# Recurrence of the HGRN2 mixer, pairs 0 and 1: four runs of small matmuls in place of seven

## What is computed

```
def chunk_step(state, inp):          # 8 heads, keys and values 128 wide
    qc, kc, vc, gc = inp             # gc = log of the forget gate
    b = jnp.cumsum(gc, axis=2)
    o_inter = einsum('bhck,bhkv->bhcv', qc * exp(b), state)
    diff = b[:, :, :, None, :] - b[:, :, None, :, :]
    decay = exp(where(causal, diff, -inf))
    scores = einsum('bhtk,bhsk,bhtsk->bhts', qc, kc, decay)
    o_intra = einsum('bhts,bhsv->bhtv', scores, vc)
    ...
```

## Time and profile before

| | us |
|---|---|
| runs | 2103.4 to 2104.62, median 2104.47 |
| profiled execution | 2104.02 |
| its span, first to last instruction | 2101.6 |
| busy in the span: PE, DVE, ACT, POOL | 2090.5, 1013.5, 742.4, 1144.2 |
| pair 0 of the recurrence | 73.9 to 113.1 |
| pair 1 | 113.1 to 157.8 |

### The profile page before, as it was taken

The page is one execution under the profiler, slowest core; times in us unless marked ns, Lnnn a source line. Parts: engine busy times, 40 slices in busy tenths (PEclk is TensorE's granted clock), DMA queues, the critical chain, the costliest instruction groups (busy, mean ns, idle before and its releaser), DMA issues.

```text
span 2101.6 us, 28243 instructions
## 1 busy us (share of the span) xinstructions
PE 2090.5 (99%) x11210; PEld 1737.6 (83%) x11210; DVE 1013.5 (48%) x1192; ACT 742.4 (35%) x862; POOL 1144.2 (54%) x821
## 2 busy tenths in 40 slices
PE   9999999999999999999999999999999999999998
PEld 7888788888888889888888888888888888888887
DVE  6367555555123365634555333744477544454126
ACT  6335542222224445533222233515433332212234
POOL 6677455555555433365555555544566555555553
PEclk9999999999999999999999999999999999999999
DMA  5212132222232222242222222222222222222321
GB/s 197 84 62 82 41 120 97 86 97 100 100 116 96 98 69 93 81 140 97 86 98 100 100 100 101 102 98 101 99 89 94 98 100 100 100 89 104 117 100 60
DMA packets 33209, 204.39 MB, mean 97 GB/s; under 512 B 3688, under 2 KB 6504, under 8 KB 9456
## 3 DMA queue, kind: packets, MB, share of 16 engines
q1 hardware_dynamic: 32896, 203.13, 28.0%
q10 hardware_dynamic: 240, 0.23, 0.0%
HBM read 200.19 MB, written 2.10 MB: 96 GB/s over the span
## 4 chain that ended last, share of the span: by engine, by line
PE 96%; DVE 2%; ACT 1%; issue 0%; DMA 0%; POOL 0%; SPq 0%; DVEq 0%; ACTq 0%
PE bank L1958 96%; DVE x L1841 0%; DMA h<-x_t 0%; DVE sgate L1890 0%; PE bank L2343 0%; ACT w_hi L776 0%; PE bank L2231 0%; DVE h L1891 0%; POOL first_wlo L721 0%; DVE ssq L1915 0%; PE bank L2370 0%; ACT sgate L776 0%; DVE aqk L1631 0%; DVE score_pair L1495 0%; ACT rstd L776 0%
## 5 line engine op out<-in xcount | busy, mean ns | idle before, releaser
L654 POOL TENSOR_TENSOR w_lo<-raw,w_hi 128x512 fp32r<-128x512 f32 x676 | 977.3, 1476 | 861.9 <-ACT w_hi L776 861.9
L1958 PE MATMUL bank<-u_hi,w_hi 128*128 128x512 f32 (+1 forms) x1936 | 753.2, 389 | 0.1
L1958 PE MATMUL bank<-u_lo,w_hi 128*128 128x512 f32 (+1 forms) x1936 | 749.5, 387 | 0.0
L776 ACT ACTIVATE w_hi<-raw 128x2048 fp32r<-128x2048 f32 x185 | 354.2, 1915 | 915.5 <-PE bank L1958 911.7
L1958 PE MATMUL bank<-u_hi,w_lo 128*128 128x512 f32 (+1 forms) x1936 | 482.2, 387 | 0.0
L1958 PEld LDWEIGHTS bank<-u_hi,w_hi 128*128 128x128 f32 x1936 | 363.6, 188 | 74.7 <-ACTq L1190 0.5
L1958 PEld LDWEIGHTS bank<-u_lo,w_hi 128*128 128x128 f32 x1936 | 363.6, 188 | 73.9 <-issue 0.2
L1958 PEld LDWEIGHTS bank<-u_hi,w_lo 128*128 128x128 f32 x1936 | 362.5, 188 | 74.6
L1958 PE MATMUL bank<-act_hi,w_hi 128*128 128x512 f32 x528 | 205.4, 389 | 0.0
L1958 PE MATMUL bank<-act_lo,w_hi 128*128 128x512 f32 x528 | 205.4, 389 | 0.0
L1329 DVE TENSOR_TENSOR h<-h,bank 128x512 f32<-128x512 f32 x48 | 30.8, 683 | 300.2 <-PE bank L1958 300.2
(11 more groups left out here) (293 smaller groups left out, 2109.2 us busy)
## 6 DMA issues: line engine op xcount, KB each, us to landing
raw<-wall SPq DMA_DIRECT2D x185, 1024.0 KB, 4.9
out_t<-h SPq DMA_DIRECT2D x8, 256.0 KB, 2.5
h<-x_t SPq DMA_DIRECT2D x3, 512.0 KB, 7.5
first_raw<-wall SPq DMA_DIRECT2D x6, 256.0 KB, 7.4
av_moved<-av SPq DMA_DIRECT2D x14, 64.0 KB, 2.1
h<-x_t SPq DMA_DIRECT2D x2, 256.0 KB, 3.9
first_raw<-wall SPq DMA_DIRECT2D x4, 128.0 KB, 3.8
lmask_f<-lmask_in SPq DMA_DIRECT2D x1, 512.0 KB
```

The source lines that it names most:

```text
L654: ins = nc.gpsimd.tensor_tensor(w_lo[:, s, c], raw[:, s, c], w_hi[:, s, c].bitcast(F32), ALU.subtract)
L776: return nc.scalar.activation(out, in_, func, **k)
L1958: return nc.tensor.matmul(out, lhsT, rhs, start=start, stop=stop, skip_group_check=True)
```

## The change

In pairs 0 and 1, levels 2 and 3, 4 and 5, and 6 and 7 each share one run on PE. The lower level of a run reads `q_dec` and `key` as before. The upper one reads two new buffers, `q_next` and `key_next`, which hold the operands of level l with the folding of level l-1 already in. `next_queries(p, l)` and `next_keys(p, l)` on VectorE make them ahead of the run: of every four quarters of a block the two that the upper level reads, one copied, one multiplied by a decay, 128x256 each. The folds in place stay, for the later levels and for the states; they now come two at a time behind the run. PE waits for both new buffers before the lower level of a run. The slices of a pair are dealt out anew, 24 as before. `key_next` is cleared once. The semaphore of the query folds is split in two, `first_dec` for the product that starts a pair and `qdec_ready` for the folds.

Cut to its core:

```diff
-LEVEL_SLICES = ((0, 4, 4, 4, 3, 3, 3, 3), (0, 4, 4, 4, 3, 3, 3, 3), (0, 4, 3, 3, 3, 3, 2, 3), (0, 3, 2, 3, 2, 2, 2, 1))
+TWO_LEVELS = 2
+LEVEL_SLICES = ((0, 3, 3, 3, 3, 4, 3, 5), (0, 3, 3, 3, 3, 4, 3, 5), (0, 4, 3, 3, 3, 3, 2, 3), (0, 3, 2, 3, 2, 2, 2, 1))
...
+        key_next = place("key_next", "a", 4, [P, 2 * S])
+        q_next = place("q_next", "a", 12, [P, 2 * S])
...
+        def levels_at(p, l):
+
+            if p >= TWO_LEVELS or l < 2:
+                return (l,)
+            return (l - 1, l) if l % 2 else ()
+
+        def next_at(p, l):
+            return (STEPS // 2 - 1) * p + l // 2
+
+        def quarters_of(t, l):
+
+            b = t.rearrange("p (n c) -> p n c", c=4 * span_of(l))
+            return [b[:, :, k * span_of(l):(k + 1) * span_of(l)] for k in range(4)]
...
+        def quarter_end(p, l, k):
+
+            t = decay_at(p, l).rearrange("p (n four) -> p n four", four=4)
+            return t[:, :, k:k + 1].to_broadcast([P, S // (2 * span_of(l)), span_of(l)])
...
             for p in range(PAIRS):
                 lo_piece(6 + 3 * p, 0, 4) if p == 0 else lo_piece(6 + 3 * p, 2, 4)
-                if p < PAIRS - 1:
+                if p < TWO_LEVELS:
+                    fold_keys(p, 1)
+                    lo_piece(7 + 3 * p, 0, 4)
+                    fold_keys(p, 2)
+                    fold_keys(p, 3)
+                    if p:
+                        head_lower(2 * p - 2)
+                    lo_piece(8 + 3 * p, 0, 4)
+                    fold_keys(p, 4)
+                    fold_keys(p, 5)
+                    decays(p + 1)
+                    lo_piece(9 + 3 * p, 0, 2)
+                    if p:
+                        head_lower(2 * p - 1)
+                    fold_keys(p, 6)
+                    fold_keys(p, 7)
+                elif p < PAIRS - 1:
...
-                tt(q_dec[p % 2][:], query[:], forget[:], ALU.mult).then_inc(qdec_ready, 1)
+                tt(q_dec[p % 2][:], query[:], forget[:], ALU.mult).then_inc(first_dec, 1)
...
                 dve.wait_ge(lev_done, 2 * STEPS * p + 2 * l + 2)
-                dve.wait_ge(qdec_ready, STEPS * p + l)
-                if l > 1:
+                if l == 1:
+                    dve.wait_ge(first_dec, p + 1)
+                else:
+                    dve.wait_ge(qdec_ready, (STEPS - 1) * p + l - 1)
                     dve.wait_ge(decay_made, (STEPS - 1) * p + l - 1)
                 high = halves_of(q_dec[p % 2], l)[1]
                 tt(high, high, ends_of(p, l)[0], ALU.mult).then_inc(qdec_ready, 1)
+
+            def next_queries(p, l):
+
+                dve.wait_ge(qdec_ready, (STEPS - 1) * p + l - 1)
+                dve.wait_ge(decay_made, (STEPS - 1) * p + l - 1)
+                to, t = quarters_of(q_next[:], l), quarters_of(q_dec[p % 2][:], l)
+                cp(to[2], t[2]).then_inc(qnext_ready, 1)
+                tt(to[3], t[3], quarter_end(p, l, 2), ALU.mult).then_inc(qnext_ready, 1)
+
+            def next_keys(p, l):
+
+                dve.wait_ge(kend_ready, (STEPS - 1) * p + l - 1)
+                dve.wait_ge(decay_made, (STEPS - 1) * p + l - 1)
+                to, t = quarters_of(key_next[:], l), quarters_of(key[p % 2][:], l)
+                cp(to[1], t[1]).then_inc(knext_ready, 1)
+                tt(to[0], t[0], quarter_end(p, l, 1), ALU.mult).then_inc(knext_ready, 1)
...
             for e in range(2):
-                ins = nc.vector.memset(scores_of_pair[e][:], 0.0)
-            ch.step(ins)
+                nc.vector.memset(scores_of_pair[e][:], 0.0)
+            ch.step(nc.vector.memset(key_next[:], 0.0))
...
+            for p in range(TWO_LEVELS):
+                fold_queries(p, 1)
+                next_queries(p, 2)
+                take_products(p)
+                take_level(p, 1)
+                next_keys(p, 2)
+                head_step(p, 1)
+                if p:
+                    gate_in(p - 1)
+                head_step(p, 2)
+                for l in (3, 5):
+                    fold_queries(p, l - 1)
+                    fold_queries(p, l)
+                    if l == 5:
+                        head_step(p, 5)
+                    next_queries(p, l + 1)
+                    take_level(p, l - 1)
+                    take_level(p, l)
+                    next_keys(p, l + 1)
+                    if l == 3:
+                        head_step(p, 3)
+                        forget_in(p + 1)
+                        head_step(p, 4)
+                        forgets(p + 1)
+                    else:
+                        keys(p + 1)
+                query_in(p + 1)
+                head_step(p, 6)
+                take_level(p, 6)
+                take_level(p, 7)
+                first_decay(p + 1)
+                head_step(p, 7)
+                if p:
+                    head_normed(2 * p - 2)
+                fold_queries(p, 6)
+                fold_queries(p, 7)
+            for p in range(TWO_LEVELS, PAIRS):
...
-                n = 2 * STEPS * p + 2 * l + a
-                q = query if l == 0 else q_dec[p % 2]
+                later = p < TWO_LEVELS and l > 1 and l % 2
+                q = query if l == 0 else q_next if later else q_dec[p % 2]
+                k = key_next if later else key[p % 2]
+                if a == 0 and p < TWO_LEVELS and l > 1:
+                    pe.wait_ge(qnext_ready, 2 * next_at(p, l))
+                    pe.wait_ge(knext_ready, 2 * next_at(p, l))
                 if a == 0 and l == 0:
                     pe.wait_ge(query_ready, p + 1)
                     pe.wait_ge(key_ready, p + 1)
-                elif a == 0:
-                    pe.wait_ge(qdec_ready, STEPS * p + l)
-                    if l > 1:
+                elif a == 0 and not later:
+                    if l == 1:
+                        pe.wait_ge(first_dec, p + 1)
+                    else:
+                        pe.wait_ge(qdec_ready, (STEPS - 1) * p + l - 1)
                         pe.wait_ge(kend_ready, (STEPS - 1) * p + l - 1)
...
-                    level(p, l, 0)
-                    level(p, l, 1)
+                    for run in levels_at(p, l):
+                        level(p, run, 0)
+                        level(p, run, 1)
```

More of the change, by code:

```diff
@@ L347, in build @@
         lev_free = sem("lev_free")
+        first_dec = sem("first_dec")
         qdec_ready = sem("qdec_ready")
+        qnext_ready = sem("qnext_ready")
+        knext_ready = sem("knext_ready")
         kend_ready = sem("kend_ready")
@@ L705, in fold_keys @@
                     pool.wait_ge(decay_made, (STEPS - 1) * p + l - 1)
+                    pool.wait_ge(kend_ready, (STEPS - 1) * p + l - 1)
                 low = halves_of(key[p % 2], l)[0]
@@ L1575, in _, with head_step @@
             for e in range(2):
-                ins = nc.vector.memset(scores_of_pair[e][:], 0.0)
-            ch.step(ins)
+                nc.vector.memset(scores_of_pair[e][:], 0.0)
+            ch.step(nc.vector.memset(key_next[:], 0.0))
             cp(sel_r[:], sel[:]).then_inc(sel_ready, 1)
             ch.settle()
-            for p in range(PAIRS):
+            def head_step(p, l):
+                if p:
+                    for e, step in HEAD_STEPS[l]:
+                        tail(2 * p - 2 + e, step)
+            for p in range(TWO_LEVELS):
[30 more added lines that the diff above has]
+                head_step(p, 7)
+                if p:
+                    head_normed(2 * p - 2)
+                fold_queries(p, 6)
+                fold_queries(p, 7)
+            for p in range(TWO_LEVELS, PAIRS):
                 for l in range(1, STEPS):
@@ L2209, in level @@
                             at = slice(CUT * b, CUT * (b + 1))
-                            ins = mm(PB[5][at, CUT * c:CUT * (c + 1)], near(key[p % 2], c)[:, at], near(q, c)[:, at])
+                            ins = mm(PB[5][at, CUT * c:CUT * (c + 1)], near(k, c)[:, at], near(q, c)[:, at])
                     elif span_of(l) >= CUT:
-                        ins = early_late_beside(l, near(key[p % 2], c), near(q, c), c)
+                        ins = early_late_beside(l, near(k, c), near(q, c), c)
                     elif span_of(l) >= LEAST_BLOCK:
                         for b in range(P // (2 * span_of(l))):
-                            ins = early_late(near(level_bank(l), c // 2), near(key[p % 2], c), near(q, c),
+                            ins = early_late(near(level_bank(l), c // 2), near(k, c), near(q, c),
                                              span_of(l), b, (c % 2) * P // 2)
@@ L2219, in level @@
                             at, to = slice(CUT * b, CUT * (b + 1)), c * P // 2 + b * CUT // 2
-                            ins = mm(level_bank(l)[at, to:to + CUT // 2], near(key[p % 2], c)[:, at],
+                            ins = mm(level_bank(l)[at, to:to + CUT // 2], near(k, c)[:, at],
                                      halves_of(near(q, c)[:, at], l)[1])
@@ L2243, in outputs @@
                 pe.wait_ge(states_ready, hd + 1)
```

(2 more changed lines are left out.)

## The result

| | before | after |
|---|---|---|
| median of the runs, us | 2103.43 | 2114.62 |
| lowest to highest (6 runs each) | 2103.21 to 2104.62 | 2108.39 to 2116.64 |
| profiled execution, its span | 2104.02, 2101.6 | 2115.07, 2113.3 |
| pair 0 of the recurrence | 39.17 | 45.29 |
| pair 1 | 44.67 | 50.20 |

The ratio is 1.0049, with a 95% interval of 1.0039 to 1.0059. The forecast was 2107.6, its range ended at 2110.6. The forecast stood on a median of 2104.47 for the kernel before, of three runs; over the six runs it is 2103.43. So the forecast change of +3.1 us is to be held against a measured +11.2. The span grew by 11.7 us, and all of it is in the two pairs that were changed: 6.12 in pair 0 and 5.53 in pair 1 (a pair is read from the start of its first `query,key` matmuls to the start of the next pair's).

A forecast was written before the change was run, and what follows sets the result against it. PE, busy 99%, was taken as the bound; -0.7 + 1.1 + 0 + 1.6 + 0.4 + 0.7 = +3.1 us on the profiled 2104.02, with 0.45 for the median, gave 2107.6, range 2104.3 to 2110.6.

The forecast's parts named there:

- merging, pair 0: Pair 0 goes from seven groups of small matmuls to four; three crossings saved, 0.72 us, at most 0.99.
- merging, pair 1: Pair 1 keeps seven groups because tail matmuls now stand alone between slices; 0 saved, bounds 0 and 0.99 us.
- places 1 and 3: PE waits before merged runs of pair 0 while DVE finishes `next_keys`: 1.1 us at run {2,3}, 1.6 at run {6,7}.
- places 2 and 4: PE waits 0 at run {4,5} of pair 0, and 0.4 us for the states at `outputs(0)` of pair 1.
- place 5: `keys_by_token(1)`, pair 1: PE waits 0.7 us for `head_taken(0)`, behind `next_keys` on DVE; 3.2 with two pieces in between.
- The price of a crossing: On PE, going from wide matmuls to small ones and back around a separate run costs 0.24 us.
- The price of the new DVE instructions: Each 128x256 copy or product costs 0.3 to 0.42 us, plus 0 to 1.27 where POOL streams.
- the fold that took 2.07: First fold of the queries on DVE, 2.07 us in place of 0.69, read as waiting for POOL's key fold.

The follow-up runs named there:

- half block: The changed kernel with three of ten warm-up matmuls replaced by 35 tiny ones, moving later PE code 128 instructions on: 2110.84 us, ratio 1.0029.
- half block with `head_taken(0)` early: The changed kernel with code moved 128 instructions on by tiny warm-up matmuls and `head_taken(0)` put ahead on DVE in pair 1: 2106.54 us, ratio 1.0008.
- `head_taken(0)` early: The changed kernel with `head_taken(0)` in pair 1 put ahead of `next_queries(1, 4)` and the two `take_level` on DVE: 2109.23 us, ratio 1.0023.
- pair 0 alone: The changed kernel with merged runs only in pair 0, pair 1 having the code of before: 2109.26 us, ratio 1.0022.
- the shifted kernel before: The kernel of before with one warm-up matmul replaced by 16 tiny ones, moving code 60 instructions on: 2104.25 us, ratio 1.0007.

## Why the prediction was wrong

Per pair, with the experiment from which each term is read:

| term | forecast | measured |
|---|---|---|
| merging, pair 0 | -0.7 | -0.8: 38.64 - 39.17 = -0.53, with 0.29 of wait in it |
| merging, pair 1 | 0 | -0.6: 44.76 - 44.67 = +0.09, with 0.65 of wait in it |
| places 1 and 3, run {2,3} and {6,7} of pair 0 | +1.1, +1.6 | +0.3, 0 |
| places 2 and 4 | 0, +0.4 | 0, 0 |
| place 5, `keys_by_token(1)` | +0.7 | +4.3 |
| slow clock behind it | not in the sum | +1.6 |
| pause inside run {2,3} | not in the sum | +3.9 |
| slow clock behind it | not in the sum | +2.4 |

The two measured pairs without losses are those of the half block (pair 0) and of the half block with `head_taken(0)` early (pair 1). The terms add up to 11.1 of the 11.65; the rest, half a microsecond, I can't place.

**What held.** The price of a crossing: 0.24 us three times is 0.72, and pair 0 without the pause saves 0.8. The price of the new DVE instructions: 0.3 to 0.43 alone and up to 1.5 beside a piece, by turns, as said of the fold that took 2.07. Which wait is new in pair 1, and its mechanism: place 5, with the sentence "If the pieces of the next panel reach POOL before `next_keys`, two of 1.27 go in between: 3.2". That is what happened, and I took 0.7.

**Place 5, a term mis-sized.** PE came when the forecast said: `outputs(0)` starts at O = 131.13 and PE arrives at 141.43 - 4.34 = 137.09, O + 6.0 (forecast O + 5.9). DVE's chain was to end at O + 6.7 and ended at O + 10.2. By its steps: the folds O + 3.0 (2.6); `next_queries` O + 4.8 (3.4), since its product lost a turn to `sum_lo`, a step of the tail that GpSimd had at 134.34 and that my chain left out; the levels O + 6.8 (5.3); `next_keys` O + 9.5 (6.0), with two pieces. The value between the ends was chosen as if the pieces were spread over the span. They start together when ScalarE has rounded the next panel, at 137.82, and `next_keys` starts at 137.88. With the upper end, which had its ground in the same trace, the forecast would have been 2110.1.

**The step that failed.** "The matmuls stay, their number and shapes too" and "The changed semaphore counts cost nothing" were read as: PE has nothing new to pay for inside a merged run. That term was put at nothing without a reason. But the trace of before has no run like these but one, levels 0 and 1, in which 256 instructions pass in 1.3 us, and I took from it that such a run is free anywhere. Whether it is depends on where the block of code ends. I gave no bound to it, from either side, and it is the largest single loss of the result, 3.9 us of waiting for code and 2.4 of slow clock behind it. The sentence that would have shown the forecast wrong, "a wait of over 2.5 us before any run of pair 0", came true inside a run instead.

**What every wait costs again.** The forecast priced a wait at its length. The two long ones cost 3.9 and 2.4, and 4.3 and 1.6, since the wide matmuls behind start 0.427 apart for a while. The experiments widen that: the pauses of 2.0 to 2.25 lost 1.2 to 1.7 us more behind them, that of 2.55 lost 2.5, those of 3.9 to 4.2 lost 1.3 to 2.5. So the second loss is 1.2 to 2.5 us whatever the length of the first. Waits up to 1.1 us, as the one of the earlier trace rows in pair 3 and the 0.65 in pair 1, have none behind them: the granted clock of those stretches is 1.00.

**Places 1, 3 and 4, each too dear.** At place 1 the mechanism held and the size did not: PE reaches run {2,3} when forecast (10.01 us from the pair's start with 0.29 of wait in it, 9.7 without; forecast 9.65), and waits for `key_next` 0.3 in place of 1.1, as `next_queries` was over half a microsecond earlier. At place 3 the profile of the half block, in which no pause hides a wait, has run {4,5} at U = 97.22 and run {6,7} at 108.20, U + 11.0 (forecast 11.1). On DVE:

```profile
101.73 2.12 DVE L1509 TENSOR_TENSOR q_dec<-q_dec,decay 128x512 f32<-128x512 f32 x2
103.89 0.59 DVE L1516 COPY q_next<-q_dec 128x256 f32<-128x256 f32 x1
104.40 0.41 DVE L1517 TENSOR_TENSOR q_next<-q_dec,decay 128x256 f32<-128x256 f32 x1
104.73 1.58 DVE L1559 COPY_PREDICATED score_pair<-lmask,bank 128x512 f32<-128x512 uint8 x2
106.21 0.27 DVE L1524 COPY key_next<-key 128x256 f32<-128x256 f32 x1
106.41 1.51 DVE L1525 TENSOR_TENSOR key_next<-key,decay 128x256 f32<-128x256 f32 x1
```

The folds are done at U + 6.6 where I had 8.3, because the wait of 1.3 for the decay product did not come, and of the four new instructions one lost a turn. `next_keys` ends at U + 10.7, 0.3 ahead of PE, where I had U + 12.7. At place 4 PE found the states ready in every profile without a pause.

**What stays open.** Why the pause seems to be missing in some runs (2102.25 of pair 0 alone, 2103.22 with `head_taken(0)` early; perhaps 2108.39 of after), and why the shifted kernel before shows none in its profile. Why the half block's runs spread over 9 us. How far ahead of its use a block is asked for, which would say in advance which runs meet a late one. A shift that costs nothing and keeps both pairs free of a pause was not found. Even so, what the change brought in the two pairs with neither loss is read off: 0.4 us of 83.84, well under what a measurement tells.

## What to carry to other kernels

When small matmuls are merged into longer runs, count instructions per microsecond and not the matmuls' time alone, and look at the longest such run of the trace as a lucky case rather than a proof. A pause in the middle of one group, with "issue" as its releaser and a packet of the instruction queue that ends a little more than 1 us before the pause does, may be code that came late; moving the code by half a block in one experiment, and by a whole one in another, tells. Where the shift is made by tiny matmuls or waits at the start, count what the start loses by them. And where PE has no waits, price a new wait of two microseconds or more at its length and 1.2 to 2.5 us on top, and take the upper end of the range if two instructions in front of the release can each lose a turn at the port.

## What the runs showed of the hardware

- PE stood 2.0 to 4.2 us in the middle of 128 small matmuls, or of the `outputs(0)` right behind them, until 1.2 to 1.45 us after the end of a packet of code of 16 KB, in all nine such pauses. In pair 0 the place is the same after a shift of 256 instructions (3.92 us both times), and after one of 128 there is no pause. With the transfer of most of a panel of 1 MB inside the pause it was 3.9 to 4.2 us, with none 2.00 and 2.55.
- Behind pauses and waits of 2.0 to 4.3 us, between about four and twelve wide matmuls started 0.427 us apart, which cost 1.2 to 2.5 us; the length of the idle time didn't order them. With the 4.3 us filled by wide matmuls, none did.
- At the start of the kernel a tiny matmul (32x16, one record of the trace) took about 0.06 us and a wait that is long met 0.023. 70 of the first in place of six records of the warm-up, and 128 of the second, moved the recurrence by 3.7 and 3.6 us, part of it by wide matmuls 0.427 apart behind them.
